# Down product of a SwiGLU in three seven-product groups, with one pair in ordinary tiles

## The reference, cut to what matters

```python
def swiglu(x, w1, w3, w2):
    return (jax.nn.silu(x @ w1) * (x @ w3)) @ w2      # w1, w3: 1024 x 2816, w2: 2816 x 1024

x = x + 0.5 * swiglu(rms_norm(x, g_ffn1), w1_ffn1, w3_ffn1, w2_ffn1)     # stage 0
z = rms_norm(x, g_mix) @ w_in + b_in                                      # the mixer
...
x = x + 0.5 * swiglu(rms_norm(x, g_ffn2), w1_ffn2, w3_ffn2, w2_ffn2)     # stage 1
gate = jax.nn.sigmoid(rms_norm(x, g_ple) @ w_ple_gate)
x = x + gate * (ple @ w_ple_proj)
```

## Time and profile before

| what | us |
|---|---|
| median of 3 runs | 949.41 (949.26 to 949.64) |
| profiled execution, its own time | 948.98 |
| its span, first to last instruction | 947.4 |
| TensorE busy | 931.6 (98%) |
| VectorE, ScalarE, GpSimd busy | 700.9, 552.3, 257.8 |

### The profile page before, as it was taken

The page is one execution under the profiler, slowest core; times in us unless marked ns, Lnnn a source line. Parts: engine busy times, 40 slices in busy tenths (PEclk is TensorE's granted clock), DMA queues, the critical chain, the costliest instruction groups (busy, mean ns, idle before and its releaser), DMA issues.

```text
span 947.4 us, 19452 instructions
## 1 busy us (share of the span) xinstructions
PE 931.6 (98%) x7750; PEld 919.9 (97%) x7750; DVE 700.9 (74%) x1164; ACT 552.3 (58%) x893; POOL 257.8 (27%) x190
## 2 busy tenths in 40 slices
PE   8999999999999999999999999999999999999997
PEld 7999999999999999889999999999999999999997
...
GB/s 247 179 101 176 143 180 149 154 162 153 158 169 109 156 89 179 73 46 67 46 78 136 112 178 145 157 172 142 157 164 150 168 164 140 140 135 89 112 24 91
DMA packets 245269, 127.62 MB, mean 135 GB/s; under 512 B 14906, under 2 KB 242580, under 8 KB 245164
## 3 DMA queue, kind: packets, MB, share of 16 engines
...
...
## 4 chain that ended last, share of the span: by engine, by line
PE 88%; DVE 5%; ACT 2%; DMA 2%; issue 1%; SPq 1%; ACTq 0%; DVEq 0%
PE ps L2011 54%; PE ps L1918 23%; PE ps L2041 6%; PE ps L2357 2%; DMA w_raw<-in_w_ffn_dram 2%; PE ps L1952 1%; DMA x_rows<-in_x_prompt_dram 1%; DVE w_lo L1616 1%; PE ps L2259 1%; PE ps L2230 0%; DVE tt L1634 0%; SPq L733 0%; ACT w_hi L810 0%; DVE w_lo L1338 0%; DVE tt L1627 0%
## 5 line engine op out<-in xcount | busy, mean ns | idle before, releaser
L2011 PE MATMUL ps<-xo_hi,w_hi 128*128 128x260 f32 x1008 | 284.5, 282 | 2.1 <-ACT snap L902 2.1
L2011 PE MATMUL ps<-xo_hi,w_lo 128*128 128x260 f32 x1008 | 284.8, 283 | 0.0
L2011 PE MATMUL ps<-xo_lo,w_hi 128*128 128x260 f32 x864 | 244.2, 283 | 0.0
L2011 PEld LDWEIGHTS ps<-xo_hi,w_hi 128*128 128x128 f32 x1008 | 189.9, 188 | 2.4 <-issue 2.4
L2011 PEld LDWEIGHTS ps<-xo_hi,w_lo 128*128 128x128 f32 x1008 | 189.9, 188 | 0.0
L1434 DVE TENSOR_TENSOR w_lo<-w_raw,w_hi 128x512 fp32r<-128x512 f32 x156 | 160.6, 1043 | 12.1 <-ACT w_hi L871 6.4
L2011 PEld LDWEIGHTS ps<-xo_lo,w_hi 128*128 128x128 f32 x864 | 162.7, 188 | 0.0
L1207 POOL DMA_DIRECT2D w_lo<-in_w_ffn_dram x52 | 66.8, 1284 | 269.0 <-ACT w_lo L878 269.0
L2011 PE MATMUL ps<-hop_hi,w_lo 128*128 128x260 f32 x448 | 126.7, 283 | 0.0
L2011 PE MATMUL ps<-hop_hi,w_hi 128*128 128x260 f32 x448 | 126.7, 283 | 0.0
L2011 PE MATMUL ps<-hop_lo,w_hi 128*128 128x260 f32 x448 | 126.5, 282 | 0.0
...
## 6 DMA issues: line engine op xcount, KB each, us to landing
w_raw<-in_w_ffn_dram SPq DMA_DIRECT2D x104, 256.0 KB, 4.4
w_lo<-in_w_ffn_dram POOLq DMA_DIRECT2D x104, 256.0 KB, 5.5
...
```

Of the source, the lines that this page charges most:

```text
L2011: ins = pe.matmul(ps[:, b, 0:Q], w[:, cc, k * P:(k + 1) * P], m_, start=(first and k == 0 and t == 0), stop=(k == kn - 1 and t == 2), skip ...
```

## The change

The down product is done in three groups of pairs instead of two: 0 to 3, 4 to 6 and 7 to 9. Only pair 10 is left to the eight ordinary tiles, which have two k-steps (12 matmuls) each. There are 30 units a stage. The first three units of the last group stand behind the first up unit of pair 10, the fourth behind the second. The three-pair units work on weight blocks of 384 columns instead of 512. The weights of the ordinary tiles are two tiles of 1024 columns instead of four of 1536. The tail is written anew; the slots of the weight tiles and the PSUM banks are permuted to suit.

```diff
-LAST_DOWN_BANKS = ((6, 1), (0, 1), (2, 3), (6, 1), (0, 1), (2, 1), (0, 1), (2, 1))
-DN_CHUNKS = ((0, 1, 2, 3), (4, 5, 6, 7))
-LAST_PAIRS = (8, 9, 10)
+LAST_DOWN_BANKS = (((6, 1), (0, 1), (4, 1), (2, 1), (6, 1), (0, 1), (4, 1), (2, 1)),
+                   ((6, 1), (0, 1), (4, 1), (2, 1), (0, 1), (2, 1), (0, 1), (6, 1)))
+P_BANK = (6, 4)
+DN_CHUNKS = ((0, 1, 2, 3), (4, 5, 6), (7, 8, 9))
+LAST_PAIR = 10
...
-            UNITS += tuple(("dn", chunk_, i) for i in range(KD // 2))
+            UNITS += tuple(("dn", chunk_, i) for i in range(KD // 2 - (pair_ == LAST_PAIR)))
     UNITS += (("up", pair_, 1),)
+UNITS += (("dn", len(DN_CHUNKS) - 1, KD // 2 - 1),)
...
-                q = [[], [("hi", "last", 0)], [("lo", "last", 0)], [("hi", "last", 1)], [("lo", "last", 1)]]
+                q = [[], [], [("hi", "last", 0)], [("lo", "last", 0)], [("hi", "last", 1)]]
+                put(n, "f", ("lo", "last", 1), ("hi", "next", 0), ("lo", "next", 0))
...
-            n, p = N_UNIT - 1, KF // 2 - 1
-            steps += [("down_a", 0), ("comb", n), ("prod", n, 4)]
-            steps += [("down_a", 1), ("h", p), ("h_hi", p), ("down_a", 2), ("h_lo", p)]
-            between = {1: [("hi", "last", 2)], 2: [("lo", "last", 2)], 3: [("hi", "last", 3)], 4: [("lo", "last", 3)],
-                       5: [("lo", "next", 0)]}
-            behind = {4: [("hi", "next", 0), ("p_turn", 0)], 5: [("hi", "next", 1), ("p_turn", 1)],
-                      6: [("lo", "next", 1), ("p_split",), ("hi", "next", 2)], 7: [("p_split_lo",), ("lo", "next", 2)]}
-            for m in range(KD):
-                steps += [("down_b" if m < 3 else "down", m), ("x_add", m)]
-                steps += between.get(m, []) + [("x_lo", m)] + behind.get(m, [])
+            n = N_UNIT - 1
+            steps += [("down", 0), ("comb", n), ("prod", n, 4), ("x_add", 0), *finish(n), ("down", 1), ("x_add", 1)]
+            behind = {3: [("p_turn", 0)], 4: [("p_turn", 1)], 5: [("p_take", 0), ("hi", "next", 1), ("lo", "next", 1)],
+                      6: [("p_take", 1), ("p_split",)]}
+            for m in range(2, KD):
+                steps += [("down", m), ("x_lo", m - 2), ("x_add", m)] + behind.get(m, [])
+            steps += [("x_lo", 6), ("x_lo", 7), ("p_split_lo",), ("hi", "next", 2), ("lo", "next", 2)]
...
+                elif m < 7:
+                    pe.wait_ge(x_ready, 16 + (2, 4, 5)[m - 4])
+                else:
+                    pe.wait_ge(p_ready, 2)
```

More of the change, by code:

```diff
@@ L575, in w_at @@
         def w_at(t, key):
-            c, n = cell[key], 2 * LAST_K // 4 if key[0] == "last" else KD // 4
-            return t[:, c:c + n, :].rearrange("p a c -> p (a c)")
+            c = cell[key]
+            return t[:, c:c + 2, :].rearrange("p a c -> p (a c)")
         def k_tiles(n):
@@ L1531, in ffn_stage @@
                         x_lo(2 * s + 1, *arg)
[L1532 removed]
+                    elif kind == "p_take" and s:
                         k, = arg
                         dve.wait_ge(p_turned, k + 1)
[L1535 removed]
+                        take_turned(p_t[:, k, :], k).then_inc(p_ready, 1)
                     elif kind == "p_split_lo" and s:
@@ L2038, in down @@
                     for n, (w, m_) in enumerate(((wh, hop_hi), (wh, hop_lo), (wl, hop_hi))):
                         for h in range(2):
-                            row = (B21, B22)[h] if k % 2 else (B11, T1)[h]
+                            row = (B21, B22)[h] if k else (B11, T1)[h]
                             ins = pe.matmul(ps[:, bank + step * h, 0:HALF], w[:, cc, w0:w0 + P],
-                                            m_[:, H_SLOT[p], row, :], start=(k == 0 and n == 0),
-                                            stop=(k == LAST_K - 1 and n == 2))
@@ L2044, in down @@
-                if part != 0:
-                    ins.then_inc(unit_done, 1)
+                                            m_[:, H_SLOT[LAST_PAIR], row, :], start=(k == 0 and n == 0),
+                                            stop=(k == 1 and n == 2))
+                ins.then_inc(unit_done, 1)
             def first_stat_out():
```

103 lines of the change are left out of this document (42 added, 61 removed).

## The result

| | before | changed |
|---|---|---|
| median of 4 runs, us | 949.46 (949.26 to 949.64) | 957.78 (954.89 to 959.30) |
| ratio, 95% interval | | 1.0081 (1.0058 to 1.0104) |
| profiled execution, its own time | 948.98 | 954.89 |
| its span | 947.4 | 953.1 |
| mean granted clock | 0.999 (the profiled one) | 0.998, 0.995, 0.993, 0.992 |

The forecast was 954.0 us (945.5 to 958.5), slower by 0.5%. The execution that was profiled is the shortest of the four. The other three took 2.7 to 4.4 us more, at a lower mean clock, and nothing in the prediction speaks of that; the last experiment does.

A forecast was written before the change was run, and what follows sets the result against it. TensorE, busy 931.6 of 947.4 us, was taken to bound the kernel: 948.98 - 5.8 - 2.6 + 0.4 + 8.1 + 4.4 = 953.5 us for an execution like the profiled one, 954.0 for the median; range 945.5 to 958.5.

The forecast's parts named there:

- Part 1: Down product: 336 more matmuls in units, 384 fewer in ordinary tiles, net 48 fewer at 0.120 us; -5.8 us.
- part 2: In front of the tail: TensorE's old waits for a saved product and for low weights are gone; -2.6 us.
- Part 3: Three-pair units: preparation is tighter but fits, second save slightly late; +0.4 us, ends 0 and 9 us.
- Rival (c): Three-pair units bound by preparation: ACT's second save late by 0.3 us in 16 units; +5, giving 958; chance 0.15.
- Part 4: Last product 4: waits for `comb` behind VectorE's split, blocked by GpSimd; 2.4 us, or 0.8 if the load lands later.
- T: Time origin for the tails: the end of product 7 of the last unit.
- Part 5: Tail of stage 0: square-and-sum loop 2.1 us a tile against TensorE's 1.44, ACT's loads late; +8.1 us with product 4's wait.
- Part 6: Tail of stage 1: tile 7 waits 2.7 us on `p_ready`, then the projection for the embedding's low part; +4.4 us.
- Rival (a): Tails keep pace: they cost only a product-4 and a tile-7 wait, 1.5 us a stage; 944 us, chance 0.22.
- Rival (b): Only ACT's load list is off: third mixer product starts with 2 us less or no wait; 950.5 us, chance 0.20.

The follow-up runs named there:

- the last experiment: The kernel before, with TensorE made to wait three times per feed-forward stage, far from the tails, for GpSimd memsets; 968.22 us, 19.1 more than the kernel before.
- the second set: The changed kernel run again with nothing edited, against the kernel before; 955.48 us (954.48 to 958.30), ratio 1.0070.
- gently: Changed kernel with two square buffers, `comb` earlier, keys' copy on VectorE, tile 7 in other banks, mixer's first product waiting for `x_add` 5; 948.73 us, ratio 1.0000.
- the copy alone: Changed kernel with only the copy of the turned keys moved from ACT to VectorE; 954.02 us, ratio 1.0045.

## Why the prediction was right

The sign and the place of the loss were right, and so was its size in the profiled execution (954.89 for 953.5). That closeness is in part luck: the tails' waits were 10.9 us for 12.5, while 1.3 us of waiting at the start, where nothing was changed, and 1.0 us that has no row came in on the other side. The median of the runs lay 3.8 us above the forecast and 0.7 below the end of the range; what carried it there, and what took it back to 955.48 in the second set, isn't in the prediction.

- **Part 1** (-5.8) and **part 2** (-2.6) are shown: 7702 matmuls, and the old waits in front of the tail are in none of the profiles.
- **Part 3** (+0.4): the first profile has one wait of 0.9 us, for the DMA that adds into a low part, which the prediction didn't have. The wait that it did have, for the second save, is in eight of the eleven later profiles, once each, of 0.2 to 1.0 us (0.6 in the changed kernel's second). So the size was right and the mechanism is seen. Rival (c), 0.3 us in each of 16 units, is ruled out: TensorE is at 100.00 of 100 us in each stretch from 100 to 300 and 600 to 800, and from 300 to the tail it waits once.
- **Part 4** (2.4, or 0.8 if the load lands late): both branches were seen, 2.8 to 3.1 and 1.1 us. The first is mis-sized, since GpSimd's split ran from T+0.8 and not from T+0.0 (342.62 with T at 341.87). In stage 1 it was 1.1 for 0.8. The profiled execution took the cheaper branch in stage 0, but this saved little: the tail's waits were 7.1 us with it and 8.5 without.
- **Part 5** (+8.1 with part 4): 7.1 us. The waits stood elsewhere than forecast. The next product could start at T+15.9 by the prediction, with 1.5 us for a low part at its seventh k-step; it started at T+16.8 (360.36 - 343.61), behind 2.8 us for an addition to x, and the low part cost 0.7, at the eighth. The cause is the one named: VectorE's additions are held up by its own blocked low parts. The loop of 2.1 us a tile was 2.13, from the start of a sum to the next. ACT's list began 22.2 us behind T (365.82 - 343.61) for 22.9 forecast, and the third product 34.0 for 34.2. Of the cause, the prediction named the buffer and VectorE's blocking; of the two, the second buffer gave 4.2 us, and with it the two engines' meeting still kept a tile at 1.74 us. The Trainium skill (SBUF — State Buffer, section Who interferes with whom) says that when VectorE reads two tiles of SBUF and GpSimd reads SBUF too, the one that issues first holds the shared ports for its whole length and the other blocks. The rows agree where VectorE comes second: 3.20 us for a split of 1.22, ending 1.08 us behind GpSimd's.
- **Part 6** (+4.4): 3.8 us. The wait on `p_ready` was 2.2 for 2.7. But the step that gave it as a price of its own failed: with other banks it was worth nothing, since the low parts of x came 2.1 us after TensorE could use them. It was right to carry the sum on to the last low part rather than to stop at tile 7.
- **Rival (a)**, tails that keep pace, is ruled out by sums 2.13 us apart and 10.9 us of waits in the tails; even the best of the cured kernels ("gently") is at 1.0000, not faster. **Rival (b)**: the list began when forecast and took 11.7 us to the end of the copy for 11.3; the copy alone was worth 1.5 us, as one of several losses.
- **What was missing** is the clock. The prediction priced each wait at its length. In nine of the twelve profiles of the table the clock was at half for 3.4 or 6.8 us at or behind a wait in a tail, up to 1.7 or 3.4 us of work each time. Three falls more would be 5 us; the three longer runs of the changed kernel have 2.7 to 4.4. That this is what made them longer is argued, not shown: they have no profile, and in the second set a run at a mean clock of 0.993 took 955.0 us and one at 0.998 took 958.3. Part of the spread is also before the tails: T was 343.61 in one profile of the changed kernel and 341.87 in the other.

What stays open: when a wait brings a fall. Behind the waits of 1.9 us and more in full stretches it did in 4 of 4, in the tails of the changed kernel's two profiles in 1 of 6 (2.8, 2.5, 2.2; 3.1, 2.4, 2.2), and in the "gently" profile behind waits of 0.6 and 1.3 us that are 1 us apart. And up to 1.2 us between the table's sums and the spans have no row.
